# Decoder step with PEER experts: the dense passes over the expert values divided anew among blocks and column halves

## The chip, the cores and the metric

One core of one Trainium2 chip runs the whole program. The metric is the device time of one execution in microseconds (us). The profile is one further execution, taken by the hardware profiler; the engines are named as in its page: PE (TensorE), PEld (its weight loads), DVE (VectorE), ACT (ScalarE), POOL (GpSimd) and SP (SyncE). SP, ACT and POOL also issue transfers, each through a queue of its own.

## The reference

One layer for 512 prompt tokens and 32 sample tokens, D = 2048. The first sub-layer (dilated attention and a spatial gate, then an output projection) gives `x1`. The change is about the second, PEER: each token chooses, for 8 heads, 16 of 16384 experts, takes the dot product of its normalised row with their rows of `expert_u`, and adds up their rows of `expert_v`:

```python
def peer_ffn(h, w_query, sub_keys, expert_u, expert_v):
    ...
        idx = jnp.take_along_axis(cand_i, best_j, axis=-1)
        gate = jax.nn.softmax(best_s, axis=-1)
        u = expert_u[idx]
        act = jax.nn.gelu(jnp.einsum('thkd,td->thk', u, hb).astype(jnp.float32), approximate=False)
        coef = (gate * act).astype(hb.dtype)
        return jnp.einsum('thk,thkd->td', coef, expert_v[idx])
...
    x = x + gt2 * ffn
```

and a final RMSNorm gives `y`.

## The kernel before

The tokens are five blocks: 0 to 3 are 128 prompt tokens each, and the last holds the 32 samples. Each engine has its own program, written out in Python; engines wait for each other on semaphores.

**Steps.** DVE's loop runs over 544 steps `s` (128 slots for each prompt block, 32 for the samples). POOL gathers, for each step, one row of `expert_u` for every token (`L2448`, 128 rows of 8 KB, 1.05 MB), up to four steps ahead (`RING = 4`), and DVE takes the dot product (`L2183`). For blocks 3 and 4 (from slot `GATHERED = 384` on) the expert's value row is gathered too, 24 steps later, also up to four ahead, and DVE adds it into `acc` (`L2096`). So from step 408 on, a step takes two gathers.

**Dense part.** Blocks 0 to 2 (`DENSE = 3`) don't gather values. Their coefficients are scattered into a matrix of tokens by all 16384 experts (`build_dense`: DVE makes one-hot rows at `L2067`, ACT scales and copies, PE multiplies at `L1015`; 32 quads to a block; the result goes to `dense_coefs` in memory), and PE multiplies it by the whole of `expert_v` (`tile_of_block`, `L1023`). A tile is 128 experts by one half of the columns: 512 KB, read in rows of 4 KB (`L2349`). The six sums (three blocks, lower and upper columns) take two of the eight PSUM banks each. The coefficients of four tiles are one chunk (`L2342`): per partition 4 KB for two blocks, 6 KB for three, 2 KB for one. SP issues tiles and chunks in one order, six tiles (`V_DENSE`) and three chunks (`C_RING`) ahead; PE frees them with `tile_used`.

The order of the tiles is the list `TILES`, of (half, i, blocks): lower columns of blocks 0 and 1 for tiles 0 to 63 (block 2 has no coefficients yet), lower columns of all three for 64 to 127, lower columns of block 2 for 0 to 63, then upper columns of all three for all 128. Sums of both halves don't fit into the banks as they are laid out, so DVE empties the lower ones in between (`end_low`).

**Order of the work on an engine.** Side programs are merged into the loop by hand-written due times: each piece yields the step at which it is due (`T_LOW`, `T_HIGH`, `C_FROM`, `t_tile`), and `side.upto(s)` issues all pieces that are due after step `s`. These times set only the order on each engine; what a piece waits for are its semaphores, and as an engine works in order, everything behind it waits too. On DVE, `end_low` stands after step 474 and `end_high` after step 534; `end_high` waits for the last tile, gates the sums and adds them to `x1` (`L2102`, `L2103`), which ACT has read back into `h2` at step 402 (`reload`).

Of the kernel before, what the change touches and what calls it, by code (L numbers as in the profile page):

```python
# [14 lines left out]
P = 128  # L15
# [111 lines left out]
EARLY_TILES = 64  # L127
# [7 lines left out]
def dense_order():  # L135

    everyone, early = range(DENSE), range(DENSE - 1)
# [6 lines left out]
TILES = dense_order()  # L144
N_LOW = NKEY + EARLY_TILES
CHUNK_AT = [m for m in range(len(TILES)) if TILES[m][1] % JS == 0]
CHUNK_OF = [sum(1 for a in CHUNK_AT if a <= m) - 1 for m in range(len(TILES))]
assert EARLY_TILES % JS == 0
# [89 lines left out]
C_FROM = [131.0, 258.0, 385.5]  # L238
# [7 lines left out]
def t_tile(m):  # L246
    if m < EARLY_TILES:
        return t_quad(1, QUADS) + 3.0 + (C_FROM[2] - t_quad(1, QUADS) - 4.0) * m / EARLY_TILES
    return t_quad(2, QUADS) + 2.0


T_LOW = 474
T_HIGH = 534
T_X1 = 402
# [36 lines left out]
def trunk_step(nc, x_prompt, x_sample, cache_k, cache_v, c_prompt, c_sample, w_ada, b_ada, g_norm1, w_in,  # L291
# [3 lines left out]
    with ctx:  # L295
# [79 lines left out]
        dense_v = [at(VD0 + HALF * i, HALF) for i in range(V_DENSE)]  # L375
        u_slot = [at(R0 + D * i, D) for i in range(RING)]
# [192 lines left out]
        def _(pe):  # L569
# [462 lines left out]
            def dense():  # L1032
                for m in range(N_LOW):
                    yield t_tile(m)
                    if m == 0:
                        pe.wait_ge(quad_taken, QUADS * (DENSE - 1))
                        pe.wait_ge(scb_copied, 6 * PH)
                        pe.wait_ge(qry_copied, 4 * PH - 2)
                    if m == EARLY_TILES:
                        pe.wait_ge(quad_taken, QUADS * DENSE)  # L1040
# [5 lines left out]
                for b in range(DENSE):  # L1046
                    if b:
                        pe.wait_ge(low_free, 2 * b)
                    for m in range(N_LOW, N_LOW + V_DENSE):
                        tile_loaded(m)  # L1050
                        ins = tile_of_block(m, b)
                        if b == DENSE - 1:
                            ins.then_inc(tile_used, 1)
                for m in range(N_LOW + V_DENSE, len(TILES)):
                    tile_loaded(m)
                    for b in range(DENSE):
                        ins = tile_of_block(m, b)
# [8 lines left out]
            pe.wait_ge(low_free, 2 * DENSE)  # L1066
            pe.wait_ge(fin_sq[1], 2)
# [9 lines left out]
        def _(act):  # L1077
# [364 lines left out]
            def reload():  # L1442
                yield T_X1
                act.wait_ge(u_done, GATHERED)
                act.wait_ge(norm_h, 10)
                act.wait_ge(x1a_stored, 32)
                act.wait_ge(x1b_stored, 48)
                for b in range(DENSE):
                    act.dma_start(h2[b], x1_of[b]).then_inc(x1_back, 16)
# [32 lines left out]
            def finish(b, s):  # L1482
# [6 lines left out]
                if after == LAG + 3:  # L1489
                    if b == SB:  # L1490
                        A.activation(stat[0:NS, 95:96], stat[0:NS, 0:1], ACT.Sqrt)
                    else:
                        act.wait_ge(low_free, 2 * DENSE)
                    for i in range(2):
# [3 lines left out]
                        square(b, i, v_slot[i][0:NS, 0:HALF] if b == SB else ps[:, 0:2, :].rearrange("p a n -> p (a n)"))  # L1498
# [5 lines left out]
            def end_high():  # L1504
                for b in range(DENSE):
# [4 lines left out]
                    square(b, 0, at(VD0 + D * (b % 2), D))  # L1510
# [24 lines left out]
        def _(dv):  # L1535
# [562 lines left out]
            def end_half(half, b):  # L2098
                for c in range(2):
                    cols = slice(half * HALF + c * NC, half * HALF + (c + 1) * NC)  # L2100
                    sums = ps[:, BANK[half, b] + c, :]
                    link(V.tensor_tensor(sums, sums, gate2_kept[:, cols], ALU.mult))  # L2102
                    ins = V.tensor_tensor(h2[b][:, cols], h2[b][:, cols], sums, ALU.add)  # L2103
                    if half == 0:
                        ins.then_inc(low_free, 1)
                    else:
                        ins.then_inc(fin_x[0], 1)

            def end_low():
# [46 lines left out]
            def end_high():  # L2156
                for b in range(DENSE):
# [3 lines left out]
                    end_half(1, b)  # L2161
# [7 lines left out]
            side = Side(choices(), gates(), norm1_b(), mix_b(), attention_b(), sample_scores(), project_out(), build_dense(), end_low(), end_high())  # L2169
# [25 lines left out]
        def _(sp):  # L2195
# [310 lines left out]
```

## Time and profile before

| | us |
|---|---|
| median of 3 runs | 3900.97 (3899.39 to 3904.64) |
| the profiled execution, its own time | 3906.27 |
| its span in the profile | 3904.5 |
| PE busy / DVE busy / POOL busy | 3097.5 / 2351.1 / 1004.5 |

The span runs from the first to the last instruction. Busy time is a sum over stages; what holds the end is read from the chain of waits and from the stretches below.

### The profile page before, as it was taken

The numbers are of one execution on the slowest core, as the hardware profiler recorded it, in microseconds if no ns is written. First come the engines' busy times: TensorE is split into PE (matmuls) and PEld (weight loads), VectorE is DVE, ScalarE is ACT, GpSimd is POOL, SyncE is SP. The second block draws the span as 40 slices with busy tenths as digits, with TensorE's granted clock in tenths as the row PEclk, the third lists the DMA queues.
The fourth block names the chain that finished last, engine by engine and source line by source line (L and its number), as shares of the span: only waits on it lengthen the run. The fifth ranks groups of instructions, "written<-read, shape, count | busy, mean of one in ns | idle before, by whom it ended". The sixth has DMA issues, their size and how long they took to land.

```text
span 3904.5 us, 28730 instructions
## 1 busy us (share of the span) xinstructions
PE 3097.5 (79%) x9975; PEld 1850.6 (47%) x9975; DVE 2351.1 (60%) x3580; ACT 571.7 (15%) x1365; POOL 1004.5 (26%) x779
## 2 busy tenths in 40 slices
PE   4999997888994677796867881499975799999950
PEld 1333444733332433345655551377742477777730
DVE  3100215889977744468987679766687386562048
ACT  0000201121112444212340002400000000000010
POOL 3000001243343411233213234222232152221015
PEclk8999998989997788897978995599998999999975
DMA  9999547989997899898979998799999999998337
GB/s 316 399 359 366 196 183 261 347 329 411 361 382 273 332 413 380 323 363 325 336 270 404 416 416 322 273 417 417 417 416 415 356 407 416 417 417 345 142 138 303
DMA packets 326129, 1344.80 MB, mean 344 GB/s; under 512 B 27625, under 2 KB 76777, under 8 KB 217593
## 3 DMA queue, kind: packets, MB, share of 16 engines
q0 software_dynamic: 106912, 749.72, 48.2%
q1 hardware_dynamic: 166090, 549.84, 36.8%
q10 hardware_dynamic: 52984, 43.42, 3.4%
q8 instruction: 80, 1.31, 0.1%
q14 instruction: 63, 0.52, 0.0%
HBM read 1303.07 MB, written 38.96 MB: 344 GB/s over the span
## 4 chain that ended last, share of the span: by engine, by line
PE 56%; DMA 21%; DVE 15%; issue 5%; ACT 2%; POOL 1%; SPq 0%; DVEq 0%; ACTq 0%; POOLq 0%
PE ps L1023 26%; PE ps L619 7%; DMA arena<-in_expert_u_dram,arena 7%; DVE arena L2183 6%; PE ps L828 6%; DMA arena<-in_expert_v_dram 5%; PE ps L778 4%; DMA arena<-in_cache_k_dram 3%; PE ps L710 3%; DMA arena<-in_w_in_dram 2%; PE ps L577 2%; DMA arena<-in_w_ada_dram 2%; PE ps L607 2%; PE ps L1015 1%; DVE arena L2067 1%
## 5 line engine op out<-in xcount | busy, mean ns | idle before, releaser
L1023 PE MATMUL ps<-arena 128*128 128x512 f32 x3072 | 1380.4, 609 | 176.9 <-DMA arena<-in_expert_v_dram 120.5
L2183 DVE CUSTOM_DVE_ANT_0 arena<-arena 128x2048 f32<-128x2048 f32 x544 | 1241.1, 2289 | 315.8 <-DMA arena<-in_expert_u_dram,arena 310.9
L2448 POOL DMA_INDIRECT arena<-in_expert_u_dram,arena x544 | 756.6, 1391 | 1974.5 <-DVE arena L2183 1787.3
L1023 PEld LDWEIGHTS ps<-arena 128*128 128x128 f32 x3072 | 943.1, 309 | 613.3 <-issue 269.0
L2096 DVE SCALAR_TENSOR_TENSOR arena<-arena 128x2048 f32<-128x2048 f32 x158 | 371.5, 2351 | 167.6 <-issue 162.3
L828 PE MATMUL ps<-arena 128*128 128x512 f32 x896 | 409.2, 610 | 0.4 <-DVE arena L2027 0.2
L577 PE MATMUL ps<-arena 128*128 128x128 f32 (+3 forms) x954 | 159.3, 320 | 179.2 <-DMA arena<-in_cache_k_dram 58.4
L2448 POOL DMA_INDIRECT arena<-in_expert_v_dram,arena x160 | 205.2, 1282 | 360.7 <-DVE arena L2096 314.8
L619 PE MATMUL ps<-arena 128*128 128x512 f32 x640 | 289.5, 606 | 7.7 <-DMA arena<-in_w_in_dram 7.6
L828 PEld LDWEIGHTS ps<-arena 128*128 128x128 f32 x896 | 169.6, 194 | 244.6 <-issue 235.6
L1405 ACT ACTIVATE arena<-arena 128x8 f32<-128x8 f32 x68 | 14.4, 211 | 1626.3 <-DVE arena L2183 1626.1
L577 PEld LDWEIGHTS ps<-arena 128*128 128x128 f32 (+3 forms) x954 | 128.8, 169 | 247.6 <-issue 84.2
L1015 PE MATMUL ps<-arena 128*128 128x128 f32 x768 | 147.9, 359 | 116.0 <-ACT arena L1424 115.9
L778 PE MATMUL ps<-arena 128*128 128x288 f32 (+1 forms) x896 | 216.0, 403 | 2.4 <-DMA arena<-in_w_query_dram 1.5
L1015 PEld LDWEIGHTS ps<-arena 128*128 128x128 f32 x768 | 133.1, 261 | 148.4 <-ACT arena L1424 134.8
L619 PEld LDWEIGHTS ps<-arena 128*128 128x128 f32 x640 | 120.4, 193 | 173.1 <-issue 173.1
L778 PEld LDWEIGHTS ps<-arena 128*128 128x128 f32 x896 | 173.3, 195 | 40.7 <-issue 2.7
L1087 ACT ACTIVATE arena<-ps 128x512 f32<-128x512 f32 (+5 forms) x255 | 127.7, 535 | 325.7 <-PE ps L577 314.6
L2102 DVE TENSOR_TENSOR ps<-ps,arena 128x512 f32<-128x512 f32 x12 | 8.3, 693 | 259.3 <-PE ps L1023 259.3
L1424 ACT ACTIVATE arena<-arena 128x128 f32<-128x128 f32 x384 | 122.3, 390 | 169.7 <-DVE arena L2067 169.1
L607 PE MATMUL ps<-arena 128*32 128x512 f32 x768 | 107.5, 671 | 48.0 <-DMA arena<-in_w_ada_dram 43.6
L2067 DVE TENSOR_TENSOR arena<-arena 128x1024 f32<-128x1024 f32 x96 | 116.3, 1220 | 34.5 <-PE ps L1015 30.0
(246 smaller groups left out, 1748.6 us busy)
## 6 DMA issues: line engine op xcount, KB each, us to landing
arena<-in_expert_v_dram SPq DMA_DIRECT2D x320, 512.0 KB
arena<-in_w_ada_dram SPq DMA_DIRECT2D x96, 1024.0 KB, 10.8
arena<-in_w_in_dram SPq DMA_DIRECT2D x80, 1024.0 KB, 8.9
arena<-in_w_query_dram SPq DMA_DIRECT2D x36, 1024.0 KB
arena<-dense_coefs SPq DMA_DIRECT2D x48, 768.0 KB
arena<-in_w_out_dram SPq DMA_DIRECT2D x32, 1024.0 KB, 5.1
dense_coefs<-arena ACTq DMA_DIRECT2D x12, 2048.0 KB, 13.5
arena<-in_cache_k_dram SPq DMA_DIRECT2D x24, 1024.0 KB
```

The lines of the kernel that those rows point to most:

```text
L577: ins = TT(ps[0:cols, bank, at_col:at_col + rows], src, ident[0:rows, 0:rows])
L607: ins = MM(ps[QUAD * j:QUAD * j + QUAD, 4, :], c_t[:, k, :], w[:, j, :], start=(k == 0), stop=(k == KD - 1))
L619: ins = MM(ps[:, banks[b], :], h_ta[:, 4 * q + k, b * P:(b + 1) * P], w[:, k, :], start=(q + k == 0), stop=(q + k == 6))
L778: ins = MM(ps[:, 2 + o, 0:n], w[:, k, o * P:(o + 1) * P], lhs[:, 4 * q + k, 0:n], start=(q + k == 0), stop=(q + k == 6))
L828: ins = MM(ps[:, b, :], lhs[:, 4 * q + k, cols_b(b)], w[:, k, :], start=(q + k == 0), stop=(q + k == 6))
L1015: ins = MM(ps[:, n % 2, i * P:(i + 1) * P], one_hot[n % 2][:, 1, i * P:(i + 1) * P], one_hot[n % 2][:, 0, i * P:(i + 1) * P], start=True, ...
L1023: ins = MM(ps[:, BANK[half, b] + c, :], weights, dense_v[m % V_DENSE][:, c * NC:(c + 1) * NC], start=(m == FIRST_TILE[half, b]), stop=(m = ...
L1087: turn_taken(A.activation(dst, src, func), key)
L2067: V.tensor_tensor(one_hot[n % 2].rearrange("p i (t n) -> p i t n", n=P), iota_key.unsqueeze(1).unsqueeze(1).broadcast_to(wide), slot_t[:, ...
L2096: V.scalar_tensor_tensor(out=acc, in0=value, scalar=scale, in1=acc, op0=ALU.mult, op1=ALU.add).then_inc(add_done, 1)
L2183: V.tensor_tensor_reduce(out=u_slot[s % RING], in0=u_slot[s % RING], in1=h2[b], scale=1.0, scalar=0.0, op0=ALU.mult, op1=ALU.add, accum_ou ...
L2448: nc.gpsimd.indirect_dma_start(out=slot, out_offset=None, in_=table, in_offset=bass.IndirectOffsetOnAxis(ap=idx, axis=0),).then_inc(loaded ...
```

## The change

The list of tiles becomes: lower columns of blocks 0 and 1 for all 128 tiles, and then for each tile i first its lower columns for block 2 and right behind them its upper columns for all three blocks. Each step of the second part reads two tiles, with one chunk of three blocks for every four i. Between the parts ACT copies the lower sums of blocks 0 and 1 from PSUM to `h2`, which frees their banks; the second part uses all eight. `end_low` is gone: `end_block` on DVE gates and adds lower and upper columns of a block together, after step 520 (`T_HIGH`) in place of 534. `x1` is read back by SP, at the end of its program, once the last tile is used.

```diff
-    order = [(0, i, early) for i in range(EARLY_TILES)]
-    order += [(0, i, everyone) for i in range(EARLY_TILES, NKEY)]
-    order += [(0, i, range(DENSE - 1, DENSE)) for i in range(EARLY_TILES)]
-    return order + [(1, i, everyone) for i in range(NKEY)]
...
+TILES = [(0, i, (0, 1)) for i in range(NKEY)]
+N_LOW = len(TILES)
+TILES += [(half, i, ((2,), (0, 1, 2))[half]) for i in range(NKEY) for half in range(2)]
...
-BANK = {(0, 0): 2, (0, 1): 4, (0, 2): 0, (1, 0): 6, (1, 1): 2, (1, 2): 4}
+BANK = {(0, 0): 2, (0, 1): 4, (0, 2): 0, (1, 0): 2, (1, 1): 4, (1, 2): 6}
...
-C_FROM = [131.0, 258.0, 385.5]
+C_FROM = [131.0, 258.0, 390.5]
...
-T_LOW = 474
-T_HIGH = 534
-T_X1 = 402
+    if m < N_LOW:
+        return t_quad(1, QUADS) + 3.0 + (C_FROM[2] - t_quad(1, QUADS) - 1.0) * m / N_LOW
+    return t_quad(2, QUADS) + 3.0
...
+T_LOW = t_quad(2, QUADS) + 1.5
+T_HIGH = 520
...
             def reload():
-                yield T_X1
...
+                yield T_LOW
+                act.wait_ge(u_done, 2 * SLOTS)
+                act.wait_ge(tile_used, N_LOW)
+                for b in range(2):
+                    sums = ps[:, BANK[0, b]:BANK[0, b] + 2, :].rearrange("p a n -> p (a n)")
+                    A.copy(h2[b][:, 0:HALF], sums).then_inc(low_free, 1)
...
+            def end_block(b):
+                for half in range(2):
+                    cols = slice(half * HALF, (half + 1) * HALF)
+                    sums = ps[:, BANK[half, b]:BANK[half, b] + 2, :].rearrange("p a n -> p (a n)")
+                    if half == 0 and b < 2:
+                        sums = h2[b][:, cols]
+                        dv.wait_ge(low_free, b + 1)
                     link(V.tensor_tensor(sums, sums, gate2_kept[:, cols], ALU.mult))
...
+                    V.tensor_tensor(h2[b][:, cols], x1_dense[b][:, cols], sums, ALU.add).then_inc(fin_x[0], 1)
...
+            sp.wait_ge(tile_used, len(TILES))
+            sp.wait_ge(x1a_stored, 32)
+            sp.wait_ge(x1b_stored, 48)
+            for b in range(DENSE):
+                sp.dma_start(x1_dense[b], x1_of[b]).then_inc(x1_back, 16)
```

On PE, around the building of block 2's coefficients, the program before has 64 tiles of two blocks (four matmuls each), then the three transposes, the 32 quads and the rest:

```order
L1015 MATMUL ps<-arena 128x128 x44
L1023 MATMUL ps<-arena 128x512 x256
L1006 MATMUL ps<-arena 128x128 x3
L1015 MATMUL ps<-arena 128x128 x128
L1023 MATMUL ps<-arena 128x512 x1280
```

The changed program has at the same place (line numbers of the changed file: `L1005` the quads, `L1013` the tiles, `L996` the transposes):

```order
L1005 MATMUL ps<-arena 128x128 x44
L1013 MATMUL ps<-arena 128x512 x504
L996 MATMUL ps<-arena 128x128 x3
L1013 MATMUL ps<-arena 128x512 x4
L1005 MATMUL ps<-arena 128x128 x4
L1013 MATMUL ps<-arena 128x512 x4
L1005 MATMUL ps<-arena 128x128 x124
L1013 MATMUL ps<-arena 128x512 x1024
```

So 126 of the 128 early tiles now stand ahead of block 2's transposes and quads, where 64 stood; 1024 matmuls follow them, where 1280 did.

On DVE the wait for the last tile now stands behind step 520, with these pieces of `end_block` between the following steps (`L2156` is the dot product, `L2076` the add, `L2085` and `L2086` the gate and the sum):

```order
L2156 ISA arena<-arena 128x2048 [waits u_loaded0,gelu_done]
L2156 ISA arena 128x1
L2058 TENSOR_TENSOR arena<-arena 128x8 [waits gelu_done]
L2076 SCALAR_TENSOR_TENSOR arena<-arena 128x2048 [waits add_done,v_loaded0,coef_done]
L2085 TENSOR_TENSOR arena<-arena 128x1024 [waits x1_back,low_free,kept_loaded,tile_used]
L2086 TENSOR_TENSOR arena<-arena 128x1024 [waits dve_step]
L2085 TENSOR_TENSOR ps<-ps,arena 128x1024
L2086 TENSOR_TENSOR arena<-arena,ps 128x1024 [waits dve_step]
```

Before, the same wait stood behind step 534, over columns in pieces of 512 and without `x1_back`:

```order
L2183 ISA arena<-arena 128x2048 [waits u_loaded2]
L2183 ISA arena 128x1
L2096 SCALAR_TENSOR_TENSOR arena<-arena 128x2048 [waits add_done,v_loaded2,coef_done]
L2102 TENSOR_TENSOR ps<-ps,arena 128x512 [waits tile_used]
L2103 TENSOR_TENSOR arena<-arena,ps 128x512 [waits dve_step]
```

Between the two orders it has moved ahead of 14 dot products and 14 adds.

## Rows read from the trace of the kernel before

**Rows 1.** the page's head, span and instructions

```profile
span 3904.5 us, 28730 instructions
```

**Rows 2.** the chain of work that ended last: start us, us, engine, line, count

```profile
2539.12 331.32 PE ps L1023 x768
...
3149.55 613.22 PE ps L1023 x1428
```

**Rows 3.** timeline of TensorE, 2040 to 2350: start us, us, what, idle before

```profile
2067.72 60.25 PE L1023 MATMUL ps<-arena 128*128 128x512 f32 x136 [23.19 <-DMA arena<-dense_coefs]
2130.24 15.16 PE L1023 MATMUL ps<-arena 128*128 128x512 f32 x32 [2.27 <-DMA arena<-in_expert_v_dram]
...
2318.58 26.51 PE L1023 MATMUL ps<-arena 128*128 128x512 f32 x56 [3.23 <-DMA arena<-in_expert_v_dram]
```

**Rows 4.** timeline of TensorE, 2900 to 3110

```profile
2937.23 5.95 PE L1023 MATMUL ps<-arena 128*128 128x512 f32 x8 [4.89 <-DMA arena<-in_expert_v_dram]
2944.80 2.08 PE L1023 MATMUL ps<-arena 128*128 128x512 f32 x4 [1.63 <-DMA arena<-in_expert_v_dram]
2948.59 2.08 PE L1023 MATMUL ps<-arena 128*128 128x512 f32 x4 [1.71 <-DMA arena<-in_expert_v_dram]
2955.54 3.42 PE L1023 MATMUL ps<-arena 128*128 128x512 f32 x4 [4.88 <-DMA arena<-in_expert_v_dram]
...
3073.00 37.34 PE L1023 MATMUL ps<-arena 128*128 128x512 f32 x86 [0.57 <-DMA arena<-in_expert_v_dram]
```

**Rows 5.** stretches of 50 us: us, PE, PEld, DVE, ACT, POOL busy, clock, DMA, GB/s

```profile
2750.00:2800.00 50.00, 50.00 (x118) 35.88 (x117) 31.39 (x31) 1.50 (x2) 11.33 (x12) 1.00 1.02 416
...
2950.00:3000.00 50.00, 26.50 (x42) 11.79 (x40) 38.73 (x62) 3.08 (x5) 16.55 (x14) 0.86 1.02 415
...
3350.00:3400.00 50.00, 50.00 (x118) 35.86 (x118) 28.96 (x20) 0.21 (x1) 11.32 (x12) 1.00 1.02 417
...
3650.00:3700.00 50.00, 50.00 (x118) 35.84 (x118) 0.00 (x0) 0.00 (x0) 0.00 (x0) 1.00 0.38 137
```

**Rows 6.** DMA queues, 3150 to 3550: packets, MB, share

```profile
q0 software_dynamic: 14797, 107.76, 65.2%
q1 hardware_dynamic: 14333, 57.45, 35.4%
```

**Rows 7.** timeline of VectorE: dot products of steps 344, 360, 416, 520; the stop at 474

```profile
2258.38 2.29 DVE L2183 CUSTOM_DVE_ANT_0 arena<-arena 128x2048 f32<-128x2048 f32 x1 [2.78 <-DMA arena<-in_expert_u_dram,arena]
...
2318.59 2.29 DVE L2183 CUSTOM_DVE_ANT_0 arena<-arena 128x2048 f32<-128x2048 f32 x1 [0.85 <-DMA arena<-in_expert_u_dram,arena]
...
2599.93 2.29 DVE L2183 CUSTOM_DVE_ANT_0 arena<-arena 128x2048 f32<-128x2048 f32 x1 [1.48 <-DMA arena<-in_expert_u_dram,arena]
...
3102.58 0.70 DVE L2102 TENSOR_TENSOR ps<-ps,arena 128x512 f32<-128x512 f32 x1 [57.00 <-PE ps L1023]
3103.32 0.69 DVE L2103 TENSOR_TENSOR arena<-arena,ps 128x512 f32<-128x512 f32 x1
...
3448.52 2.29 DVE L2183 CUSTOM_DVE_ANT_0 arena<-arena 128x2048 f32<-128x2048 f32 x1 [1.47 <-DMA arena<-in_expert_u_dram,arena]
```

**Rows 8.** timeline of TensorE and SyncE, 2404 to 2562

```profile
2411.10 0.87 PE L1006 MATMUL ps<-arena 128*128 128x128 f32 x3 [66.01 <-issue]
...
2529.13 1.55 SPq L2342 DMA_DIRECT2D arena<-dense_coefs  x3
```

**Rows 9.** timeline of all engines, 3740 to 3905

```profile
3762.80 0.70 DVE L2102 TENSOR_TENSOR ps<-ps,arena 128x512 f32<-128x512 f32 x1 [202.34 <-PE ps L1023]
...
3816.20 2.28 DVE L2183 CUSTOM_DVE_ANT_0 arena<-arena 128x2048 f32<-128x2048 f32 x1
...
3820.67 2.28 DVE L2183 CUSTOM_DVE_ANT_0 arena<-arena 128x2048 f32<-128x2048 f32 x1
...
3890.11 1.22 DVE L2145 TENSOR_TENSOR ps<-ps,arena 32x1024 f32<-32x1024 f32 x1 [3.81 <-PE ps L1072]
```

**Rows 10.** reads of x_mid, 2500 to 3850: issue to landing

```profile
DMA to landing us min/median/max: 6.4/8.3/10.2
```

More of the change, by code:

```diff
@@ L132 @@
 assert VD0 + V_DENSE * HALF <= Z0
-def dense_order():
-    everyone, early = range(DENSE), range(DENSE - 1)
-    order = [(0, i, early) for i in range(EARLY_TILES)]
-    order += [(0, i, everyone) for i in range(EARLY_TILES, NKEY)]
-    order += [(0, i, range(DENSE - 1, DENSE)) for i in range(EARLY_TILES)]
-    return order + [(1, i, everyone) for i in range(NKEY)]
-TILES = dense_order()
-N_LOW = NKEY + EARLY_TILES
-CHUNK_AT = [m for m in range(len(TILES)) if TILES[m][1] % JS == 0]
+TILES = [(0, i, (0, 1)) for i in range(NKEY)]
+N_LOW = len(TILES)
+TILES += [(half, i, ((2,), (0, 1, 2))[half]) for i in range(NKEY) for half in range(2)]
+CHUNK_AT = [m for m in range(len(TILES)) if TILES[m][1] % JS == 0 and (m < N_LOW or TILES[m][0] == 0)]
 CHUNK_OF = [sum(1 for a in CHUNK_AT if a <= m) - 1 for m in range(len(TILES))]
-assert EARLY_TILES % JS == 0
 FIRST_TILE = {(h, b): min(m for m, t in enumerate(TILES) if t[0] == h and b in t[2]) for h in range(2) for b in range(DENSE)}
 LAST_TILE = {(h, b): max(m for m, t in enumerate(TILES) if t[0] == h and b in t[2]) for h in range(2) for b in range(DENSE)}
-BANK = {(0, 0): 2, (0, 1): 4, (0, 2): 0, (1, 0): 6, (1, 1): 2, (1, 2): 4}
+BANK = {(0, 0): 2, (0, 1): 4, (0, 2): 0, (1, 0): 2, (1, 1): 4, (1, 2): 6}
 NEAR = CH - FAR
@@ L375, in trunk_step @@
         dense_v = [at(VD0 + HALF * i, HALF) for i in range(V_DENSE)]
+        x1_dense = [at(CB0 + D * b, D) for b in range(DENSE)]
         u_slot = [at(R0 + D * i, D) for i in range(RING)]
@@ L1045, in dense @@
                 yield t_tile(N_LOW)
[L1046 to L1054, printed above, removed]
+                pe.wait_ge(quad_taken, QUADS * DENSE)
+                for m in range(N_LOW, len(TILES)):
                     tile_loaded(m)
-                    for b in range(DENSE):
+                    for b in TILES[m][2]:
+                        if m == N_LOW + 1 and b < 2:
+                            pe.wait_ge(low_free, b + 1)
                         ins = tile_of_block(m, b)
@@ L1492, in finish @@
                     else:
-                        act.wait_ge(low_free, 2 * DENSE)
+                        act.wait_ge(idx_ready, heads_of(SB, PH))
                     for i in range(2):
@@ L1497, in finish @@
                             act.wait_ge(fin_sq[1], 1)
-                        square(b, i, v_slot[i][0:NS, 0:HALF] if b == SB else ps[:, 0:2, :].rearrange("p a n -> p (a n)"))
+                        square(b, i, v_slot[i][0:NS, 0:HALF] if b == SB else at(TK0, HALF))
                 if after == LAG + 4:
@@ L2167, in end_high @@
                     scale_rows(b)
-            side = Side(choices(), gates(), norm1_b(), mix_b(), attention_b(), sample_scores(), project_out(), build_dense(), end_low(), end_high())
+            side = Side(choices(), gates(), norm1_b(), mix_b(), attention_b(), sample_scores(), project_out(), build_dense(), end_high())
             dv.wait_ge(norm_h, 4)
@@ L2335, in load_chunk @@
             def load_chunk(u):
-                half, i, blocks = TILES[CHUNK_AT[u]]
-                parts = slice(4 * blocks[0], 4 * blocks[-1] + 4)
+                m = CHUNK_AT[u]
+                blocks = 2 if m < N_LOW else DENSE
                 if u >= C_RING:
@@ L2340, in load_chunk @@
                 for n in range(2):
-                    sp.wait_ge(stage_stored[n], 8 * 4 * (blocks[-1] + 1))
-                sp.dma_start(dense_c[u % C_RING][:, GRP_T * parts.start:GRP_T * parts.stop, :].rearrange("p t j -> p (t j)"),
-                             c_dram[i // JS, :, parts, :].rearrange("p g x -> p (g x)")).then_inc(c_loaded[u % C_RING], 16)
+                    sp.wait_ge(stage_stored[n], 16 * 2 * blocks)
+                sp.dma_start(dense_c[u % C_RING][:, 0:P * blocks, :].rearrange("p t j -> p (t j)"),
+                             c_dram[TILES[m][1] // JS, :, 0:4 * blocks, :].rearrange("p g x -> p (g x)")).then_inc(c_loaded[u % C_RING], 16)
             def load_tile(m):
@@ L2349, in load_tile @@
                 sp.dma_start(dense_v[m % V_DENSE], v_rows[i * NKEY:(i + 1) * NKEY, half * HALF:(half + 1) * HALF]).then_inc(dv_loaded[m % V_DENSE], 16)
-            loads = [(CHUNK_AT[max(u - C_RING + 1, 0)] + V_DENSE - 1 if m < EARLY_TILES else
-                      max(CHUNK_AT[max(u - C_RING + 1, 0)], EARLY_TILES) + V_DENSE - 1, 0, u) for u, m in enumerate(CHUNK_AT)]
+            loads = [(max(CHUNK_AT[max(u - C_RING + 1, 0)], N_LOW * (m >= N_LOW)) + V_DENSE - 1, 0, u) for u, m in enumerate(CHUNK_AT)]
             loads += [(m, 1, m) for m in range(len(TILES))]
```

38 lines of the change are left out of this document (5 added, 33 removed).

## The prediction

> **What bounds the kernel now.** I began with the chain of waits. From 2539 us on it is nearly all TensorE multiplying coefficients by expert values (L1023), with reads of the value tiles in the middle; the last of these stretches runs from 3149.55 for 613.22 us, to 3762.8 [rows 2]. Then VectorE takes up its work again: its timeline shows it idle for 202.34 us before that moment, released by L1023 [rows 9]. So `end_high` stops VectorE behind step 534 (3762.80 less 202.34 is 3560), and with it the gathers: in 3650 to 3700 the memory traffic is 137 GB/s, against 417 in 3350 to 3400 [rows 5]. From 3762.8 to the end of the span at 3904.5 [rows 1] there are 141.7 us of tail: nine dot products, 33 adds, the three dense blocks' ends and the samples' end. The end is therefore **the last tile plus what VectorE still has behind its stop**.
>
> Next I asked what paces the tiles. In the stretches where three blocks use each tile, PE is busy 50.00 of 50 us, 118 matmul records, so 0.424 us each [rows 5]; a matmul in the program is two such records, so a tile costs 3.39 us for two blocks, 5.08 for three, 1.69 for one. With two blocks it is not PE: the timeline has gaps that end with the arrival of a tile, and from 2130.24 to 2318.58 ten groups of four tiles went by, 18.83 us a group, 4.71 a tile [rows 3]. With one block it is far off: tiles come 3.79 us apart and a group takes 18.31 (2937.23 to 2955.54) [rows 4], PE busy 26.50 of 50 [rows 5].
>
> These intervals say how the memory traffic is divided while gathers run. A group early on is four tiles and a chunk in rows of 4 KB, 2.62 MB in 18.83 us: 139 GB/s, a third of 417. The tiles 3.79 us apart are 139 GB/s too. A gather's rows are 8 KB. In the one-block stretch the chunk, 262 KB in rows of 2 KB, takes what is left, 18.31 - 4 x 3.79 = 3.15 us: 83 GB/s, a fifth of 417. So the tile queue gets its share row by row: 4 of 12, 2 of 10. It is not served by need.
>
> The Trainium skill ("DMA: Bandwidth & Descriptors", the part "SWDGE vs HWDGE vs iDMA") says that an engine takes turns between its queues, switching between packets of preferably at most 4096 B. By that alone both queues would get the same bytes, 208 GB/s each, and tiles would come 2.5 us apart; the rows above show 3.79, so the measurement decides, and the rule is only the rival below.
>
> **The change, stage by stage.** Matmuls are unchanged in number (1536 in the program, 3072 records). Tile reads grow from 320 to 384 (64 x 0.524 = 33.6 MB more), chunks shrink by 8.4 MB: 25 MB more, 60 us at 417 GB/s, if nothing else hid it.
>
> *First part, two blocks.* It starts as before (2067.72; 17 tiles by 2130.24 [rows 3]) but has 128 tiles instead of 64. VectorE goes on at (2318.59 - 2258.38)/16 = 3.76 us a step [rows 7] and reaches step 392, where the first quads of block 2 are due, at 2258.4 + 48 x 3.76 + 2.3 = 2441. PE by then has 17 + (2441 - 2130)/4.71 = 83 tiles. The order shows that block 2's transposes stand behind tile 125, so VectorE waits for them, and behind it all gathers. The remaining 45 tiles now run at PE's own pace, 8 records of 37.34/86 = 0.434 us [rows 4]: 156 us, plus 4 for the four gathers still in the ring. Low columns end near **2601**. Before, the transposes ran at 2411.10 [rows 8]: this is 190 us later.
>
> *Building block 2's coefficients* took from 2411.10 [rows 8] to the first tile at 2539.12 [rows 2], 128 us. Behind it ACT's reads of `x1` (3 MB) leave this place; its two copies come in, each one pass over 1024 columns, near the price of L2103 doubled, 2 x 0.69 [rows 7], beside the store and the first chunks (issued at 2529.13 [rows 8]). I take 125 us (between 110, if the reads delayed the first chunks by all of their share, and 130): second part from **2726**.
>
> *Second part.* For four i it takes 64 records, 27.1 us of PE. Its reads are eight tiles, 8 x 3.79 = 30.3 us at the share above, and a chunk of 0.786 MB in rows of 6 KB. Its share is not shown by a row of its own; by the same division 6 of 14 of 417, 179 GB/s, 4.4 us. Bounds: 3.8 (the 4 KB chunk's time for half more data) and 6.0 (the 2 KB chunk's rate, at most doubled time). Also the three-block stretches, four tiles and such a chunk, would be 19.6 us by this, under PE's 20.3, and PE shows no gap there. So 34.7 us a group, **PE waits for tiles** while gathers run.
>
> Gathers then have 417 - 5.0/34.7 = 273 GB/s, a step 2 x 1.05 MB, 7.7 us; the gather queue measured 107.76 MB in 400 us, 269 GB/s, with PE at full pace [rows 6]. Before, 104 steps from 416 to 520 took 3448.52 - 2599.93, less 57.00 and 8 us for the stop at 474 [rows 7]: 7.5 each. Step 416 comes 61 us after the first tile (2599.93 less 2539.12), at 2787, and step 520 at 2787 + 104 x 7.7 + 5 = **3593**. There VectorE stops; eight gathers in the rings last 31 us more. Till 3624 the reads had 898 us and a head start of three chunks (13 us) and six tiles: 911/34.7 x 8 + 6 = 216 of 256 tiles. The other 40 go at 3.39: **last tile at 3760**. That is where it is now (3762.8): the removed stop at 474 and the missing one-block stretch are spent again at 392 and on waits for tiles.
>
> *The tail.* `x1` is only now read, 3 x 1.05 MB at 417 GB/s and a start: one such read took 6.4 to 10.2 us to land [rows 10], beside gathers; I take 10 for three alone (8 to 16). Behind the stop VectorE has 14 more dot products and adds than before. Their gathers are 14 x 2 x 1.05/0.417 = 70.4 us; VectorE itself needs 4.47 a pair (3816.20 to 3820.67 [rows 9]), 63, so memory sets it. Ending the blocks was 12 pieces at 0.69 [rows 7] and is 12 of 1024 columns at 1.22 [rows 9], 6 us more. Sum: 3760 + 10 + 141.7 + 70.4 + 6 = **3988** of span. The profiled execution took 3906.27 for a span of 3904.5, and the median of the runs is 5.3 below it: 3988 + 1.8 - 5.3, about **3985**, 2.2% slower.
>
> **Rivals.** (a) *The tile queue gets what PE needs* (at least 184 GB/s in the second part). Then PE is the bound from 2726: 256 x 3.39 = 868 us, last tile 3594, 169 us earlier than now. Gathers keep 233 GB/s, 9.0 us a step, and are at step 506 then; 14 more at 5.03 make 3666, and no stop comes. With the same tail of 218 us: span 3884, median 3881, 0.5% faster. This is what the skill's rule of equal packets would bring. For it: PE never waits in today's three-block stretches, though their need is 142 GB/s, so the share may exceed 142. Against it: both stretches in which PE does wait sit at exactly a third. 10 in 100.
>
> (b) *The second part is faster than my division, but not PE-bound.* With a group of 31 us, 235 + 6 tiles are in by 3624, 15 remain, last tile 3675: the span is 3904, no change. That asks for 160 GB/s. No row is near. 5 in 100.
>
> (c) *The large chunks cost their upper bound*, 36.3 us a group: 207 tiles in, 49 remain, last tile 3790, span 4018, median 4015. TensorE's granted clock, 0.86 where it waits for tiles [rows 5], may add a few us at each return to full pace; the row at 3073.00 shows 0.434 us a record there against 0.424. 10 in 100.
>
> My forecast (a stop at 392, waits for tiles, a stop at 520, 3940 to 4005) has 75 in 100. A measurement of this kernel tells about 0.2% from no change; (b) is split around it. Slower 0.85, within 0.2% 0.05, faster 0.10. The range leaves out (a) and most of (b) and takes in (c): 3920 to 4025.
>
> **What the new profile would show.** A stop of VectorE and of the gathers of about 155 us before the transposes (2441 to 2601), ended by TensorE's tiles; memory traffic near 190 GB/s in it. In the second part groups of 64 records every 34.7 us with gaps ended by the value tiles, PE busy about 39 of 50 us. A second stop near 3593 for 170 to 180 us, and about 228 us from the last tile to the end. If PE shows 118 records in 50 us from 2750 on, (a) is right. What would break it otherwise: a step rate behind 416 far from 7.7, or VectorE passing step 392 without a wait.

## The result, and the profile after

| | before | after |
|---|---|---|
| median of the runs of this comparison, us | 3902.8 (3899.39 to 3909.08, 4 runs) | 3995.89 (3985.69 to 4001.33, 4 runs) |
| ratio after to before, 95% interval | | 1.0234 (1.0208 to 1.0259) |
| the profiled execution's own time, and its span | 3906.27, 3904.5 | 3985.69, 3983.9 |

The change makes the kernel 2.3% slower. The time of 3995.9 us lies 11 us above the forecast of 3985 and inside its range of 3920 to 4025.

The page of the kernel after: the span, the two large DMA queues, and the groups of TensorE's dense matmuls (L1013, the line that was L1023), of VectorE's one-hot operations for block 2 (L2047), and the reads.

```profile
span 3983.9 us, 28807 instructions
...
q0 software_dynamic: 106912, 749.72, 47.2%
q1 hardware_dynamic: 173434, 578.15, 38.3%
...
L1013 PE MATMUL ps<-arena 128*128 128x512 f32 x3072 | 1422.0, 624 | 217.4 <-DMA arena<-in_expert_v_dram 180.4
...
L2047 DVE TENSOR_TENSOR arena<-arena 128x1024 f32<-128x1024 f32 x96 | 116.6, 1220 | 185.7 <-ACT arena L1395 157.1
```

The 3072 matmul records are the same in number as before. They wait 180.4 us for value tiles.

The timeline of VectorE shows the step places that answer to [rows 7, 9]: the dot products of step 392 (2434.99), 416 (2756.68) and 520 (3570.16), and the two operations at which it had stopped (2587.03 and 3771.26; in brackets the idle time and what ended it).

```profile
2434.99 2.29 DVE L2156 CUSTOM_DVE_ANT_0 arena<-arena 128x2048 f32<-128x2048 f32 x1 [0.86 <-DMA arena<-in_expert_u_dram,arena]
...
2587.03 2.36 DVE L2047 TENSOR_TENSOR arena<-arena 128x1024 f32<-128x1024 f32 x2 [149.66 <-ACT arena L1395]
...
2756.68 2.29 DVE L2156 CUSTOM_DVE_ANT_0 arena<-arena 128x2048 f32<-128x2048 f32 x1 [1.50 <-DMA arena<-in_expert_u_dram,arena]
...
3570.16 2.29 DVE L2156 CUSTOM_DVE_ANT_0 arena<-arena 128x2048 f32<-128x2048 f32 x1 [1.48 <-DMA arena<-in_expert_u_dram,arena]
...
3771.26 1.23 DVE L2085 TENSOR_TENSOR arena<-arena 128x1024 f32<-128x1024 f32 x1 [194.94 <-DMA arena<-x_mid]
```

The first stop names a ScalarE copy (L1395) as its releaser. That copy had itself waited for TensorE's transposes of block 2, and those stood behind the low tiles: the timeline of TensorE shows it at 2585.99. In the same view the second part begins at 2690.89, its groups of 64 records follow one another every 34.7 us, each start released by a value tile, and the last stretch is unbroken.

```profile
2443.51 142.64 PE L1013 MATMUL ps<-arena 128*128 128x512 f32 x328 [3.79 <-DMA arena<-in_expert_v_dram]
2585.99 0.49 PE L996 MATMUL ps<-arena 128*128 128x128 f32 x3
...
2690.89 14.36 PE L1013 MATMUL ps<-arena 128*128 128x512 f32 x27 [13.54 <-issue]
...
2915.79 30.42 PE L1013 MATMUL ps<-arena 128*128 128x512 f32 x64 [4.71 <-DMA arena<-in_expert_v_dram]
2950.47 30.15 PE L1013 MATMUL ps<-arena 128*128 128x512 f32 x64 [4.25 <-DMA arena<-in_expert_v_dram]
2985.18 15.28 PE L1013 MATMUL ps<-arena 128*128 128x512 f32 x30 [4.56 <-DMA arena<-in_expert_v_dram]
...
3581.63 179.66 PE L1013 MATMUL ps<-arena 128*128 128x512 f32 x412 [4.08 <-DMA arena<-in_expert_v_dram]
```

The windows that answer to [rows 5] (same columns) are one in the first stop, one in the second part, one in the second stop.

```profile
2500.00:2550.00 50.00, 50.00 (x118) 35.84 (x118) 0.00 (x0) 0.00 (x0) 0.00 (x0) 1.00 0.55 188
2950.00:3000.00 50.00, 44.98 (x94) 29.20 (x95) 38.42 (x59) 1.59 (x3) 12.42 (x14) 0.88 1.02 416
3650.00:3700.00 50.00, 50.00 (x118) 35.99 (x117) 0.00 (x0) 0.00 (x0) 0.00 (x0) 1.00 0.54 179
```

In both stops TensorE runs at full pace, 118 records in 50 us, and the memory moves 188 and 179 GB/s. In the second part the DMA engines are full (share 1.02, 416 GB/s) and TensorE does 94 records: it waits. The DMA queues from 2800 to 3500, which answer to [rows 6], show how the 416 GB/s are divided; q1 carries the tiles and chunks, 99.73 MB in 700 us, 142 GB/s. The gathers are in q0 (a line gives packets, MB and the share of the 16 engines' time).

```profile
q0 software_dynamic: 25967, 189.08, 65.4%
q1 hardware_dynamic: 25952, 99.73, 35.2%
```

The two queues moved the same number of packets, 25967 and 25952, though not the same bytes. A gathered row has 8 KB, a row of q1 has 4 KB (tiles) or 6 KB (chunks).

The chain of waits (start, us, what) has the same pattern from 2863 to 3562, and then the end, which answers to [rows 2].

```profile
2950.47 14.72 PE ps L1013 x28
2965.57 19.47 DMA arena<-in_expert_v_dram
...
3581.63 179.67 PE ps L1013 x412
3762.16 8.91 DMA arena<-x_mid
```

The difference of the spans, 3983.9 - 3904.5 = 79.4 us, is therefore made of three pieces. The last tile comes at 3761.3 instead of 3762.8 [rows 9] (-1.5). VectorE waits 10.0 more for `x_mid` (3771.26 less 3761.3). From there to the end it takes 212.6 us instead of 141.7 (+70.9). Single executions also differ in when the dense work starts: at 2067.72 before [rows 3], at 2061.30 after (below). Counted from there the tiles took 1695.1 before and 1700.0 after.

```profile
2061.30 60.20 PE L1013 MATMUL ps<-arena 128*128 128x512 f32 x136 [23.25 <-DMA arena<-dense_coefs]
```

### The profile page after: what moved, and what is told of

Its sections match the earlier page's. It is cut to its first block, busy times and chain, and to the rows that moved or that the text cites. A ratio compares the mean times of both kernels' runs of the same rounds, so it can differ in the third digit from the quotient of the medians.

```text
span 3983.9 us, 28807 instructions
## 1 busy us (share of the span) xinstructions
PE 3130.4 (79%) x9975; PEld 1846.3 (46%) x9975; DVE 2351.0 (59%) x3568; ACT 576.4 (14%) x1369; POOL 987.7 (25%) x779
## 4 chain that ended last, share of the span: by engine, by line
PE 48%; DMA 30%; DVE 13%; issue 4%; ACT 2%; POOL 1%; SPq 1%; DVEq 0%; ACTq 0%; POOLq 0%
PE ps L1013 22%; DMA arena<-in_expert_v_dram 18%; PE ps L609 7%; DVE arena L2156 5%; PE ps L818 4%; PE ps L768 4%; DMA arena<-in_cache_k_dram 3%; PE ps L700 3%; PE ps L567 2%; DMA arena<-in_expert_u_dram,arena 2%; DMA arena<-in_w_ada_dram 2%; DMA arena<-in_w_in_dram 2%; PE ps L597 2%; PE ps L1005 1%; DVE arena L2076 1%
## 5 line engine op out<-in xcount | busy, mean ns | idle before, releaser
L1013 PE MATMUL ps<-arena 128*128 128x512 f32 x3072 | 1422.0, 624 | 217.4 <-DMA arena<-in_expert_v_dram 180.4
L2156 DVE CUSTOM_DVE_ANT_0 arena<-arena 128x2048 f32<-128x2048 f32 x544 | 1241.7, 2289 | 319.1 <-DMA arena<-in_expert_u_dram,arena 313.9
L1013 PEld LDWEIGHTS ps<-arena 128*128 128x128 f32 x3072 | 945.3, 310 | 692.1 <-issue 366.0
L2425 POOL DMA_INDIRECT arena<-in_expert_u_dram,arena x544 | 743.4, 1366 | 2067.5 <-DVE arena L2156 1877.6
L2076 DVE SCALAR_TENSOR_TENSOR arena<-arena 128x2048 f32<-128x2048 f32 x158 | 371.6, 2352 | 167.8 <-issue 161.8
L818 PE MATMUL ps<-arena 128*128 128x512 f32 x896 | 406.6, 607 | 0.4 <-DVE arena L2007 0.2
L609 PE MATMUL ps<-arena 128*128 128x512 f32 x640 | 290.1, 607 | 10.2 <-DMA arena<-in_w_in_dram 10.2
L1005 PE MATMUL ps<-arena 128*128 128x128 f32 x768 | 141.5, 346 | 112.9 <-ACT arena L1405 112.8
L2047 DVE TENSOR_TENSOR arena<-arena 128x1024 f32<-128x1024 f32 x96 | 116.6, 1220 | 185.7 <-ACT arena L1395 157.1
L1005 PEld LDWEIGHTS ps<-arena 128*128 128x128 f32 x768 | 126.6, 249 | 144.8 <-ACT arena L1405 132.1
L1053 PE MATMUL ps<-arena 128*32 128x512 f32 x8 | 7.2, 1060 | 206.0 <-DVE arena L2076 203.3
L597 PE MATMUL ps<-arena 128*32 128x512 f32 x768 | 108.0, 675 | 44.0 <-DMA arena<-in_w_ada_dram 39.6
```

The lines of the kernel that those rows point to most:

```text
L597: ins = MM(ps[QUAD * j:QUAD * j + QUAD, 4, :], c_t[:, k, :], w[:, j, :], start=(k == 0), stop=(k == KD - 1))
L609: ins = MM(ps[:, banks[b], :], h_ta[:, 4 * q + k, b * P:(b + 1) * P], w[:, k, :], start=(q + k == 0), stop=(q + k == 6))
L818: ins = MM(ps[:, b, :], lhs[:, 4 * q + k, cols_b(b)], w[:, k, :], start=(q + k == 0), stop=(q + k == 6))
L1005: ins = MM(ps[:, n % 2, i * P:(i + 1) * P], one_hot[n % 2][:, 1, i * P:(i + 1) * P], one_hot[n % 2][:, 0, i * P:(i + 1) * P], start=True, ...
L1013: ins = MM(ps[:, BANK[half, b] + c, :], weights, dense_v[m % V_DENSE][:, c * NC:(c + 1) * NC], start=(m == FIRST_TILE[half, b]), stop=(m = ...
L2076: V.scalar_tensor_tensor(out=acc, in0=value, scalar=scale, in1=acc, op0=ALU.mult, op1=ALU.add).then_inc(add_done, 1)
```

## The experiments

**Theory:** the tile queue gets its share row by row beside the gathers (as many rows as they get), so in the second part TensorE waits for tiles; and the stop at step 520 leaves fourteen more dot products and adds behind the last tile. **Rival:** the queue gets what it needs or an equal share, and the loss lies in the place of the stop alone, or in the stops themselves.

### 1 to 4: the place of the upper stop, in either order

`a534` is the kernel after with the upper stop where it stood before; `a560` has it behind nearly all steps; `b520` and `b560` are the kernel before with its stop at the same two other places.

```diff
-T_HIGH = 520      # after
+T_HIGH = 534      # a534;  560 in a560
-T_HIGH = 534      # before
+T_HIGH = 520      # b520;  560 in b560
```

a534: 

> The changed kernel with the dense blocks' end due after step 534, as before, not 520. If the order of the passes and the early place of the stop both cost (my account): the stop begins 14 steps later, 14 x 7.8 = 109 us, in which tiles come every 34.7/8 us in place of 27.1/8, so the last tile is some 24 us later, and 14 pairs of gathers, 70 us, leave the tail. Net about -46 us against the changed kernel: near 3950 us, still over 1% slower than before. Rival 1, the place of the stop is all that the change cost: back to 3903. Rival 2, the place doesn't matter: 3996 as the changed kernel.

a560: 

> The changed kernel with the dense blocks' end due after step 560, so that VectorE hardly waits there. My account: the gathers go on during the dense tiles; the last tile moves from 3761 to about 3805 us since the tiles keep only their share, but nothing is left behind it except a few adds and the ends: span about 3870, median near 3880 us, 0.5% faster than before. Rival, the tail is bound by something else than gathers stopped early: no more than 20 us gained against the changed kernel.

b520: 

> The kernel before, with only the dense blocks' end moved from step 534 to 520. Its tiles are paced by TensorE there, so the last tile should stay at 3763 us, and 14 pairs of gathers move behind it: +66 to +70 us, near 3970 us. If the tiles gain from the gathers' stop instead (tile queue starved there too), less than that: +45.

b560: 

> The kernel before, with the dense blocks' end moved from step 534 to 560. Gathers and adds go on while TensorE multiplies; the last tile should stay near 3763 us as TensorE sets the pace with three blocks to a tile; behind it stand 8 adds, the ends of the dense blocks and of the samples, some 60 us: near 3825 us, 2% faster than before. If gathers going on slow the tiles down (share under need), the last tile comes later and the gain is under 60 us.

| | median us | ratio to before (95%) |
|---|---|---|
| a534 | 3947.03 | 1.0107 (1.0071 to 1.0144) |
| a560 | 3889.86 | 0.9962 (0.9941 to 0.9984) |
| b520 | 3959.81 | 1.0137 (1.0097 to 1.0178) |
| b560 | 3802.10 | 0.9740 (0.9699 to 0.9781) |

Expected were near 3950 (a534), 3880 (a560), 3970 (b520) and 3825 (b560). They miss by 3, 10, 10 and 23 us, and for three of them the rival is far off. For b520 the time alone does not decide: +57 us lies between the account (+66 to +70) and the alternative that the tiles gain by the earlier stop (+45). Its timeline does, below: the tiles took 1698.1 us against 1695.1.

VectorE's and TensorE's timelines of a534 (span 3945.3) show the stop and the last stretch of tiles:

```profile
3795.79 1.23 DVE L2085 TENSOR_TENSOR arena<-arena 128x1024 f32<-128x1024 f32 x1 [108.73 <-DMA arena<-x_mid]
...
3689.07 96.73 PE L1013 MATMUL ps<-arena 128*128 128x512 f32 x220 [4.65 <-DMA arena<-in_expert_v_dram]
```

and the same two views of b520 (span 3958.2):

```profile
3752.23 0.70 DVE L2102 TENSOR_TENSOR ps<-ps,arena 128x512 f32<-128x512 f32 x1 [308.78 <-PE ps L1023]
...
3062.91 689.28 PE L1023 MATMUL ps<-arena 128*128 128x512 f32 x1604 [0.73 <-DMA arena<-in_expert_v_dram]
```

Since the executions start their dense work at different moments (2054.1 in b520, 2049.1 in b560, 2063.2 in a534, 2055.7 in a560), I count from there:

| | dense start to last tile | stop's end to the end | median |
|---|---|---|---|
| before | 3762.8 - 2067.7 = 1695.1 | 3904.5 - 3762.8 = 141.7 | 3902.7 |
| b520 | 3752.2 - 2054.1 = 1698.1 | 3958.2 - 3752.2 = 206.0 | 3959.8 |
| b560 | 3745.3 - 2049.1 = 1696.2 | 3796.0 - 3745.3 = 50.7 | 3802.1 |
| after | 3761.3 - 2061.3 = 1700.0 | 212.6 | 3995.9 |
| a534 | 3785.8 - 2063.2 = 1722.6 | 3945.3 - 3795.8 = 149.5 | 3947.0 |
| a560 | 3796.5 - 2055.7 = 1740.8 | 3876.2 - 3796.5 = 79.7, from the last tile, no stop | 3889.9 |

In the old order the place of the stop changes only the tail (+64 for 520, -91 for 560): the tiles take the same 1695 to 1698 us. In the new order a later stop shortens the tail (63 us from 520 to 534) but lengthens the tiles, by 23 us and by 41, for TensorE is starved as long as gathers run. In the medians the place at 520 costs 57 us in the old order and 49 in the new one. What is left of the 93 us, 3947 against 3903, is the order itself: 44 us. At 560 the orders are 88 us apart in the medians and 80.2 in the spans: 45 of tiles (1740.8 less 1696.2), 29 of tail and 6.6 of the start. The tail is longer in a560 because VectorE still adds gathered rows when the last tile is done and comes to the dense blocks' end only at 3819.10; in b560 it had waited 63.25 us for the last tile. In b560 TensorE has no gap from 3056.29 on, in a560 it has one in nearly every group:

```profile
3056.29 688.97 PE L1023 MATMUL ps<-arena 128*128 128x512 f32 x1604 [0.16 <-DMA arena<-in_expert_v_dram]
```

```profile
3614.36 29.93 PE L1013 MATMUL ps<-arena 128*128 128x512 f32 x64 [4.62 <-DMA arena<-in_expert_v_dram]
3649.01 29.96 PE L1013 MATMUL ps<-arena 128*128 128x512 f32 x64 [4.72 <-DMA arena<-in_expert_v_dram]
...
3790.95 5.51 PE L1013 MATMUL ps<-arena 128*128 128x512 f32 x12 [0.21 <-DMA arena<-in_expert_v_dram]
```

The earlier starts of the profiled executions, 18.6 us in b560 and 13.6 in b520, are about the size of their misses of 23 and 10, but whether the starts explain the medians too is not shown.

### 5 and 6: the rows of the tile reads

`rows_2k` reads each tile of the kernel after in two DMAs with rows of 2 KB. `rows_8k` reads, in the second part, the lower and the upper tile of one i (which are neighbours in memory and in use) with one DMA in rows of 8 KB. Bytes, matmuls and order are unchanged in both. The number of transfers changes with the rows: twice as many for the tiles in `rows_2k`, half as many for the second part's in `rows_8k`.

```diff
 # rows_2k
-sp.dma_start(dense_v[m % V_DENSE], v_rows[i * NKEY:(i + 1) * NKEY, half * HALF:(half + 1) * HALF])
+for c in range(2):
+    cols = slice(half * HALF + c * NC, half * HALF + (c + 1) * NC)
+    sp.dma_start(dense_v[m % V_DENSE][:, c * NC:(c + 1) * NC], v_rows[i * NKEY:(i + 1) * NKEY, cols])
 # rows_8k
+elif (m - N_LOW) % 2 == 0:
+    sp.wait_ge(tile_used, m - V_DENSE + 2)
+    sp.dma_start(at(VD0 + HALF * (m % V_DENSE), D), v_rows[i * NKEY:(i + 1) * NKEY, :])
```

rows_2k: 

> The changed kernel with each value tile read by two transfers in rows of 2 KB instead of one in rows of 4 KB: the same bytes. If the queue's share goes row by row (2 of 10 of 417 GB/s beside gathers of 8 KB rows), a tile takes 6.3 us while gathers run instead of 3.79: the group of 64 records in the second part takes 8 x 6.3 + 4.4 = 55 us instead of 34.7, gathers run faster (6.4 us a step), the stops at 392 and 520 grow to over 200 and some 450 us, and the kernel to about 4230 us. Rival, the queues share by bytes or by need: tiles keep 3.79 us and the time stays near 3996.

rows_8k: 

> The changed kernel with both halves of a tile read by one transfer in rows of 8 KB in the second part: the same bytes, two neighbouring buffers. Row by row the tile queue then gets 8 of 16 of 417 GB/s, 209: four double tiles 20.1 us and a chunk 4.4 make 24.6, under TensorE's 27.1, so TensorE never waits in the second part: last tile 2691 + 868 = 3559 instead of 3761, gathers slow to 9.0 us a step while it runs, no stop at 520, span about 3850, median near 3865 us. Rival, share by bytes or by need: groups stay at 34.7 us and the time near 3996.

Measured: rows_2k 4235.22 us (2 runs), ratio 1.0845 (1.0822 to 1.0868); rows_8k 3862.17 us, ratio 0.9883 (0.9863 to 0.9904). Both lie within 6 us of what was expected. In rows_2k the two stops of VectorE grew to 237 and 524 us. TensorE's timeline of rows_2k in the second part, pairs of tiles (16 records):

```profile
2944.79 8.93 PE L1013 MATMUL ps<-arena 128*128 128x512 f32 x16 [3.93 <-DMA arena<-in_expert_v_dram]
2957.51 9.72 PE L1013 MATMUL ps<-arena 128*128 128x512 f32 x16 [3.80 <-DMA arena<-in_expert_v_dram]
2970.25 10.18 PE L1013 MATMUL ps<-arena 128*128 128x512 f32 x16 [3.02 <-DMA arena<-in_expert_v_dram]
```

A pair comes every 12.73 us, 6.37 a tile: 0.524 MB in that time is 82 GB/s, a fifth of 412. With rows of 4 KB it is 3.79 us, a third. The demand was the same, so the share does not go by need. Nor does it go by transfers: there were twice as many, and the share fell. The DMA queues of rows_2k from 2900 to 3300 give the measure: again both moved the same number of packets.

```profile
q0 software_dynamic: 17473, 127.24, 77.4%
q1 hardware_dynamic: 17473, 35.48, 23.2%
```

These equal counts also answer a rival that the chain of waits suggests, since it starts each tile read at the moment when TensorE frees a buffer (2965.57): that six buffers are too few. A queue that ran short of work would fall behind in packets, as it does in rows_8k below; here it does not. A kernel with more buffers was not run. How many rows one turn of a queue takes is not shown either, only that the two queues get equally many.

TensorE's timeline and the DMA queues from 2800 to 3500 of rows_8k:

```profile
2692.96 215.51 PE L1013 MATMUL ps<-arena 128*128 128x512 f32 x496 [13.90 <-issue]
2912.21 668.12 PE L1013 MATMUL ps<-arena 128*128 128x512 f32 x1552 [3.74 <-DMA arena<-in_expert_v_dram]
```

```profile
q0 software_dynamic: 22693, 165.27, 57.0%
q1 hardware_dynamic: 18176, 125.71, 43.3%
```

There is one gap in 887 us (868 had been expected), and q1 now stays behind q0 in packets, 18176 to 22693: it has its fill. q1 moves 125.71 MB in 700 us, 180 GB/s, against 142; that is about TensorE's full need (4.98 MB in 27.1 us is 184), so its share is at least this, and what it would reach with more demand is not shown. The last tile comes at 3580 instead of 3761, and no stop at 520 is left. The kernel gains 134 us by it. The rival of an equal share is out: with equal bytes, rows of 4 KB would have fed TensorE already.

### 7 to 10: the stop at step 392

A stop of 150 us remains. I let TensorE take only 80 low tiles ahead of block 2's transposes and the other 48 behind its quads, and set the upper stop to 560, with rows of 4 KB (`no_stop_392`) and of 8 KB (`rows_8k_no_stops`).

```diff
 def t_tile(m):
+    if m < AHEAD:        # AHEAD = 80
+        return t_quad(1, QUADS) + 3.0 + (C_FROM[2] - t_quad(1, QUADS) - 4.0) * m / AHEAD
     if m < N_LOW:
-        return t_quad(1, QUADS) + 3.0 + (C_FROM[2] - t_quad(1, QUADS) - 1.0) * m / N_LOW
+        return t_quad(2, QUADS) + 1.0
```

no_stop_392: 

> The changed kernel with the end of the dense blocks due after step 560 (3890 us measured), and now with only 80 of the 128 early tiles ahead of block 2's transposes on TensorE, the other 48 behind its quads, so that VectorE isn't stopped at 392. Seen alone, a stop of 150 us with the gathers at rest looks like the worst loss. My account says that it isn't one: tiles are what lasts, they go at TensorE's pace in the stop and at their share outside, and the gathers' total time at rest or in work decides how many go at which; so the time stays within 15 us of 3890. Rival, the stop at 392 is lost time: 100 us or more gained, under 3800.

rows_8k_no_stops: 

> All three together: rows of 8 KB in the second part, 80 tiles ahead of block 2's transposes, the end of the dense blocks after step 560. With the share enough for TensorE, removing stops is worth their time: transposes at 2437, the other 48 early tiles at 4.7 us till 2745, last tile at 2745 + 868 = 3613, gathers at step 530 by then, 14 pairs at 5.0 and 24 adds at 2.5 us behind, then the samples' end: span about 3770, median near 3785 us, 3% faster than before and under the 3802 of the kernel before with the late end. Rival, gathers and not tiles hold this one, and the 9 us a step leave it over 3802.

Measured: no_stop_392 3876.82 us, ratio 0.9933 (0.9908 to 0.9958); rows_8k_no_stops 3863.38 us, ratio 0.9892 (0.9875 to 0.9908), a miss of 78 us. VectorE's timeline says why; first no_stop_392, then rows_8k_no_stops:

```profile
2701.46 0.17 DVE L2063 TENSOR_TENSOR arena<-arena 128x8 f32<-128x8 f32 x1 [158.71 <-ACT arena L1391]
```

```profile
2707.08 0.17 DVE L2064 TENSOR_TENSOR arena<-arena 128x8 f32<-128x8 f32 x1 [158.18 <-ACT arena L1392]
```

The stop was not gone, it had moved to step 408: ScalarE's copies of the low columns, due at `T_LOW` (near 406), now waited for the 48 late tiles, and behind them on ScalarE stood the small activation that VectorE needs once in eight steps. The two kernels did not test what they were made for. The second pair has these copies later as well:

```diff
-T_LOW = t_quad(2, QUADS) + 1.5
+T_LOW = 433
-T_KEPT = 434
+T_KEPT = 440
```

no_stops: 

> no_stop_392 once more, with ScalarE's two copies of the low sums moved from step 406 to 433: there they waited for the 48 late tiles, and VectorE stopped at step 408 for 159 us instead of at 392, so that run kept the stop. Now neither is left. My account, the tiles last longest and their pace outside a stop is their share of the memory traffic: no gain from the 150 us, within 15 us of the 3877 and 3890 of the two kernels with the stop. Rival, the stop is lost time: under 3790.

rows_8k_no_stops_2: 

> rows_8k_no_stops with the copies moved in the same way. Its first try kept a stop of 158 us at step 408. With rows of 8 KB the tiles of the second part are paced by TensorE, so here the stop is lost time: last early tile near 2736, last tile near 3605, gathers at step 529 then, 15 pairs and 24 adds behind it: span about 3780, median near 3785 us, 80 us under the first try. Rival, it stays within 20 us of 3863: then VectorE's stop costs nothing with long rows either.

Measured: no_stops 3904.13 us, ratio 1.0005 (0.9992 to 1.0017), 27 us above no_stop_392, where I had allowed 15; rows_8k_no_stops_2 3794.99 us, ratio 0.9724 (0.9694 to 0.9754), 10 above its expectation. With rows of 4 KB, VectorE's and TensorE's timelines of no_stops (span 3908.5) show a stop again, now at the very end:

```profile
3851.39 1.23 DVE L2090 TENSOR_TENSOR arena<-arena 128x1024 f32<-128x1024 f32 x1 [174.29 <-DMA arena<-x_mid]
...
2758.24 41.95 PE L1018 MATMUL ps<-arena 128*128 128x512 f32 x92 [18.70 <-issue]
...
3690.03 151.41 PE L1018 MATMUL ps<-arena 128*128 128x512 f32 x348 [4.32 <-DMA arena<-in_expert_v_dram]
```

VectorE finished its steps early and waited 174.3 us for the last tile (3841) and the read of `x1` behind it: taking the stop of 158 us away made the kernel 27 us slower than no_stop_392. The time at full pace had only moved. In no_stop_392 the low tiles ran through in the stop and the second part began at 2701.77; in no_stops they came one every 4.7 us and it began at 2758.24, 56 us later, and the 151 us at full pace at the end won back only a part. While tiles are starved, a stop of the gathers is no loss, for the tiles go at full pace in it. With rows of 8 KB the same edit brings 68 us (3863 to 3795), and TensorE's timeline runs through:

```profile
2808.82 824.46 PE L1018 MATMUL ps<-arena 128*128 128x512 f32 x1920 [1.05 <-DMA arena<-in_expert_v_dram]
```

Its tiles end at 3633 and the gathers set the end: 26% of its chain of waits is reads of gathered value rows, and 3700 to 3750 shows no matmul. It has the lowest median here; b560, run in another comparison, lies 0.2% above it, within the intervals, so the two are not ranked. The two kernels without stops differ only in the rows of the second part.

## Why the prediction was right, step by step

The mechanism was right: two stops, tiles that wait beside the gathers, and fourteen pairs more in the tail. That the sum came within 11 us is in part luck, as the terms show.

**First part and the stop at 392.** Predicted: step 392 at 2441, low columns done at 2601, VectorE stopped for about 155 us. Measured: 2434.99, about 2594, and 149.66. This execution had begun the dense work 6 us earlier, so the intervals agree within 6 us.

**Building block 2's coefficients: mis-sized.** I took 125 us, between 110 and 130; from 2585.99 to 2690.89 it is 105, under my range. TensorE's wait behind the last quad is 13.5 us. The second part began 35 us before the predicted 2726: 20 by this term, 6 by the earlier start, and 9 because my sum put the transposes (2601) behind all 128 low tiles. The order in the program shows them behind 126, two tiles or 7 us less, and they ran at 2585.99.

**The group of 34.7 us: right.** 2915.79, 2950.47 and 2985.18 are 34.68 and 34.71 apart, and q1's 142 GB/s is the 143 that 4.98 MB in 34.7 us give. Not every group kept it: the 23 groups from 2772.19 to 3581.63 average 35.2, and the two longest took 39.6 and 37.2. Most of the excess has the size of a term that I had left out, ScalarE's own transfers through a third queue (q10). Around the longest group, from 2870 to 2916, it moved two reads for the blocks' end, 2.10 MB, which is 5.0 us at 417 GB/s, and the group took 4.9 more. The one of 37.2 met a read of `x_mid` (1.05 MB, 2.5 us), and took 2.5 more. From 2772 to 3582 this queue moved 3.44 MB, 8.2 us at 417 GB/s, and the 23 groups took 11.3 us beyond 34.7 each. No run without these transfers was made. The start was slower than I allowed, too: 20.5 tiles were used by 2772.19, where my sum has 28. These two ate the 35 us: 412 records are left at 3581.63, about 51.5 tiles, so 204.5 of 256 are used; by my numbers (216 at 3624, one every 4.34 us) it would have been 206. The errors cancelled, and that part of the agreement is luck.

**The steps of 7.7 us: right.** From 2756.68 to 3570.16 there are 104 steps, 7.82 each; step 520 came 23 us before the predicted 3593, by the early start.

**The last tiles.** I took 3.39 us each; 412 records in 179.66 us are 0.436 a record, 3.49 a tile. The window at 3650 has 0.424, so the 5 us are at the start of the stretch. Against that, the full pace began at 3581.63 and not at 3624, since step 520 came early: ten tiles at 3.49 instead of 4.34 us. Last tile 3761.3, predicted 3760.

**The tail.** `x_mid` 10.0 us as taken. The rest is 212.6 us against 141.7 + 70.4 + 6 = 218.1. The term that was mis-sized is the fourteen pairs: 63 us (after against a534) and 64 (b520 against before), not 70.4. That is 4.5 to 4.6 a pair, near VectorE's own 4.47, so the transfers did not set it, as I had said, but VectorE. The other term is 149.5 - 141.7 = 7.8 us, not 6. So the span is 3983.9 against 3988.

**From span to median: the wrong sign.** I put the median 5.3 us below the profiled execution, as before; it was 10.2 above. These 15.5 us, less the 4 by which the span was shorter, make the 11 us between forecast and result.

**Signs.** The first stop's traffic (188 GB/s), the gaps and the second stop came as forecast, the stop with 195 us, 10 of them for `x_mid`, instead of 170 to 180. TensorE's busy time did not: 45 of 50 us, where I had 39. The number of records (94) is near the 92 of a group of 34.7 us, but each lasted longer at the granted clock of 0.88.

**Rivals.** (a), that the tile queue gets what TensorE needs, fell: 94 records in 50 us, not 118, and rows_2k and rows_8k moved the share with the row while the need stayed. The Trainium skill ("DMA: Bandwidth & Descriptors", "SWDGE vs HWDGE vs iDMA") has an engine take turns between its queues, with packets of preferably at most 4096 B. Turns agree with the equal packet counts; equal bytes, as I read the rule, do not: the queue would have had 208 GB/s with rows of 4 KB, and the runs show 139, and 82 with rows of 2 KB. (b) needed groups of 31 us and fell with the same rows. (c), 36.3 us a group, was the nearer miss: the mean of 35.2 lies between my value and it, but most of the excess is the size of the third queue's traffic, not a cost of every chunk.

What stays open: where the last 3 us of the 23 groups go, why the start of the second part was slower than the sum, why the start of the dense work scatters between executions (2049 to 2071 in the twelve profiles), and whether 8 KB rows would get exactly half. None of these was tried.

## What to carry to other kernels

Before joining passes to save transfers, ask at what rate the joined pass is fed while another queue is busy: here the share of the 417 GB/s went by row size (a fifth, a third, and at least 180 GB/s for rows of 2, 4 and 8 KB beside gathers of 8 KB), and reading two neighbouring half rows in one DMA was worth 134 us. A stop of 150 us is no loss as such; it counts only if the work that goes on in it is not what ends last, so find out first what ends last (no_stops: +27 us from removing it, rows_8k_no_stops_2: -68). When a hand-written order holds an engine at a fixed step, everything behind that step falls into the tail: move that place first, alone, since one number gave the old kernel 2.6%.

## What I had not expected of the hardware

TensorE's mean granted clock is lower where it has short gaps: 0.88 in 2950 to 3000, with gaps of 4 to 5 us in every 35, and 64 records take 30.42 us (0.475 each) instead of 0.424. Over the whole kernel the same 3072 records were busy 1422.0 us, where the kernel before had 1380.4, and rows_2k 1495.5. Here that was hidden, since the next tile came later anyway: the group at 2915.79 was busy 30.42 us and the one at 3019.89 29.95, and both lasted 34.68. The division by rows also held more closely than I had thought: a tile of rows_2k took 6.37 us where it gives 6.3, and a group of rows_2k 55.3 us (2932.06 to 2987.36) where it gives 55.
